# Feed-forward up projection by one level of Strassen's method, with the gated rows kept in DRAM

## The reference

```python
def conv_ffn(h, w_up, conv_w, conv_b, w_down, rows):
    bsz, length, _ = h.shape
    u = (h @ w_up).reshape(bsz, rows, length // rows, 2 * D_FF)
    up = jnp.pad(u, ((0, 0), (0, 0), (1, 1), (0, 0)))
    u = up[:, :, :-2] * conv_w[0] + up[:, :, 1:-1] * conv_w[1] + up[:, :, 2:] * conv_w[2] + conv_b
    a, b = jnp.split(u.reshape(bsz, length, 2 * D_FF), 2, axis=-1)
    return (jax.nn.silu(a) * b) @ w_down
```

## Time and profile before

| | us |
|---|---|
| median of 3 runs (2785.47 to 2792.19) | 2789.98 |
| span of the profiled execution | 2783.0 |
| from there to the median | 7.0 |
| PE busy in the span | 2719.7 |
| DVE, ACT, POOL busy | 1490.9, 1080.5, 256.6 |
| up projection, in the span | 2056.3 to about 2537.7 |

### The profile page before, as it was taken

The page is one execution under the profiler, slowest core; times in us unless marked ns, Lnnn a source line. Parts: engine busy times, 40 slices in busy tenths (PEclk is TensorE's granted clock), DMA queues, the critical chain, the costliest instruction groups (busy, mean ns, idle before and its releaser), DMA issues.

```text
span 2783.0 us, 42406 instructions
## 1 busy us (share of the span) xinstructions
PE 2719.7 (98%) x17076; PEld 2343.7 (84%) x17076; DVE 1490.9 (54%) x2652; ACT 1080.5 (39%) x2084; POOL 256.6 (9%) x392
## 2 busy tenths in 40 slices
PE   6999999999999999999999999999999999999999
PEld 6888888888998888878887988888998888888887
DVE  5766664544446566654445485553374444545335
ACT  5444443333334444433334552223362222224232
POOL 2211100000002122000002060000030000000000
PEclk9999999999999999999999999999999999999999
DMA  4211211111321212122113241113231111111113
GB/s 151 63 63 55 78 60 60 60 58 62 131 84 46 71 64 80 60 69 81 51 65 117 67 137 46 46 46 113 84 114 54 46 52 47 46 53 54 53 61 129
DMA packets 149185, 200.11 MB, mean 72 GB/s; under 512 B 8806, under 2 KB 117030, under 8 KB 148990
## 3 DMA queue, kind: packets, MB, share of 16 engines
q1 hardware_dynamic: 128064, 134.20, 15.3%
q0 software_dynamic: 20928, 63.20, 6.3%
HBM read 162.66 MB, written 32.58 MB: 70 GB/s over the span
## 4 chain that ended last, share of the span: by engine, by line
PE 90%; DVE 4%; ACT 2%; issue 2%; DMA 1%; POOL 1%; SPq 0%; DVEq 0%; ACTq 0%; POOLq 0%
PE PS L977 85%; PE PS L986 5%; DMA T<-TMP 1%; DVE AL L2243 1%; DVE WL L2200 0%; DVE ST L2372 0%; POOL TMP L2979 0%; DVE TMP L2355 0%; DVE T L2348 0%; POOL T L2976 0%; ACT top L1769 0%; ACT TMP L1608 0%; ACT TMP L1718 0%; ACT WH L1596 0%; DVE top L2385 0%
## 5 line engine op out<-in xcount | busy, mean ns | idle before, releaser
L977 PE MATMUL PS<-AH,WH 128*128 128x512 f32 (+3 forms) x2528 | 941.1, 372 | 16.9 <-DVE AL L2243 10.2
L977 PE MATMUL PS<-AL,WH 128*128 128x512 f32 (+3 forms) x2528 | 894.2, 354 | 0.0
L977 PE MATMUL PS<-AH,WL 128*128 128x512 f32 (+3 forms) x2528 | 893.6, 353 | 0.0
L977 PEld LDWEIGHTS PS<-AH,WH 128*128 128x128 f32 x2528 | 476.5, 188 | 87.7 <-issue 18.7
L977 PEld LDWEIGHTS PS<-AH,WL 128*128 128x128 f32 x2528 | 476.0, 188 | 48.1
L977 PEld LDWEIGHTS PS<-AL,WH 128*128 128x128 f32 x2528 | 477.4, 189 | 44.5 <-issue 1.0
L2200 DVE TENSOR_TENSOR WL<-W,WH 128x1024 fp32r<-128x1024 f32 x184 | 226.0, 1231 | 221.5 <-ACT WH L1596 221.4
L977 PE MATMUL PS<-WH,AH 128*128 128x256 f32 (+1 forms) x1016 | 325.1, 320 | 1.7 <-DVE WL L2200 1.7
L977 PE MATMUL PS<-WL,AH 128*128 128x256 f32 (+1 forms) x1016 | 324.4, 319 | 0.0
L977 PE MATMUL PS<-WH,AL 128*128 128x256 f32 (+1 forms) x1016 | 324.4, 319 | 0.0
L2372 DVE TENSOR_REDUCE ST<-PS 128x1 f32<-128x784 f32 (+8 forms) x272 | 188.0, 732 | 144.4 <-PE PS L977 143.8
(11 more groups left out here) (341 smaller groups left out, 3345.7 us busy)
## 6 DMA issues: line engine op xcount, KB each, us to landing
W<-in_k_w_in SPq DMA_DIRECT2D x66, 512.0 KB, 3.8
W<-in_w_ada SPq DMA_DIRECT2D x48, 512.0 KB, 4.8
W<-in_w_up SPq DMA_DIRECT2D x44, 512.0 KB, 3.8
W<-in_w_in SPq DMA_DIRECT2D x28, 512.0 KB, 3.7
W<-in_w_out SPq DMA_DIRECT2D x24, 512.0 KB, 3.5
W<-in_w_down SPq DMA_DIRECT2D x22, 512.0 KB, 3.7
R<-s_xs POOLq DMA_DIRECT2D x16, 512.0 KB, 6.5
s_adap<-AST POOLq DMA_DIRECT2D x48, 128.0 KB, 4.7
```

The lines of the kernel that those rows point to most:

```text
L977: return e.matmul(out, lhsT, rhs, start=start, stop=stop, skip_group_check=True)
```

## The change

The up projection of one j, which was [a-half columns, b-half columns] by [token half 0, token half 1] with the input columns in two halves of 4 slices, is a 2 x 2 by 2 x 2 block product. It is done with seven block products in Winograd's form in place of eight. One block product is 4 slices k times three matmuls, 12 matmuls of 512 columns.

- **Activations.** Besides the blocks a11, a12, a22 of `BH`/`BL`, four combined blocks s1 = a21+a22, s2 = s1-a11, s3 = a11-a21, s4 = a12-s2 are formed once, each with its own high and low part. POOL makes s1, s3 and the cast of a22, DVE s2 and s4 and all low parts, ACT all other high parts (`combine_in`, `combine_hi`, `combine`, `combine_sums`, `combine_rest`), slice by slice for pairs 2 and 3, in pieces of 128 x 256 with one buffer (`CMB`) for each sum.
- **Weights.** POOL forms four differences of 128 x 512 for each j (`combine_weights`), ACT and DVE split each of the seven halves (`up_split`, `up_split_lo`) four products ahead.
- **Results.** Products 1, 6, 7, 4 of one j add up in one bank, and ACT copies its state out after 1, 6 and 7 (`snap`); 2 lies in a bank of its own; 5 and 3 share a third. DVE adds C11 = snap 1 + bank of 2 and C12 = snap 6 + bank of 3 (`total`), POOL C22 = snap 7 + snap 5 (`result`). PE may not begin 6, 7, 4, 3 before the snap of 1, 6, 7, 5. Three of four convolutions now read C11, C12 and C22 in SBUF.
- **Gated rows.** SBUF no longer holds all 22. Rows go to a ring of four slots, POOL writes rows 0 to 17 to DRAM (`gs`), and reads them back when the up projection is over; the down projection takes rows 18 to 21 first.

The core of the diff ("..." marks what is left out):

```diff
+        UP_SEQ = [(0, 1), (0, 2), (1, 1), (1, 2), (2, 1), (2, 2), (0, 5), (0, 6), (0, 7), (0, 3), (0, 4)]
+        UP_SEQ += [(j, p) for j in (1, 2) for p in (6, 5, 7, 3, 4)] + [(j, p) for j in range(3, FT) for p in (1, 2, 6, 5, 7, 3, 4)]
+        UP_AHEAD = 4
...
 # tensor
+            def product(i, j, p):
...
+                if p == 6:
+                    e.wait_ge(*up_snap.at((j, 1)))
+                elif p == 7:
+                    e.wait_ge(*up_snap.at((j, 6)))
+                elif p == 4:
+                    e.wait_ge(*up_snap.at((j, 7)))
+                elif p == 3:
+                    e.wait_ge(*up_snap.at((j, 5)))
+                e.wait_ge(*w_lo.at(("up", i)))
...
+            for i, (j, p) in enumerate(UP_SEQ):
+                product(i, j, p)
                 if i == 1:
+                    tensor_norm_fill(e, "ffn", 3, [b for b in ALL if b not in live])
...
 # scalar, end of the mixer
-                split_to(WI["up", 0, 0])
+                up_split(0)
+                up_split(1)
                 ffn_fill(1)
-                split_to(WI["up", 0, 1])
                 mix_squares(3, 3)
+                combine_in(2, 0)
                 mix_root(3)
+                combine_hi(2, 0, ("s1", "s3"))
                 sum_stats(3)
-                ffn_fill(2)
+                combine_hi(2, 0, ("s2", "s4"))
+                for k in range(1, 4):
+                    combine_in(2, k)
+                    combine_hi(2, k, ("s1", "s3"))
+                    combine_hi(2, k, ("s2", "s4"))
...
 # scalar, ffn
+                up_split(2)
+                up_split(3)
+                for i, (j, p) in enumerate(UP_SEQ):
+                    if i + UP_AHEAD < len(UP_SEQ):
+                        up_split(i + UP_AHEAD)
+                    if p == 1:
...
+                        snap(j, 1, C11)
+                        if j == 0:
+                            for k in range(4):
+                                combine_in(3, k)
+                                combine_hi(3, k, ("s1", "s3"))
+                                combine_hi(3, k, ("s2", "s4"))
...
+                        elif j >= 3:
+                            gate(j - 1)
+                    elif p == 2:
+                        if j != 2:
+                            convolve(j, 0, 0)
+                    elif p == 6:
...
+                        snap(j, 6, C12)
...
+                    elif p == 3:
+                        convolve(j, 1, 1)
+                        convolve(j, 1, 0)
+                    elif p == 4:
+                        convolve(j, 0, 1)
+                    if j == FT - 1 and p in (5, 7, 3):
+                        gated_hi((5, 7, 3).index(p))
+                gate(FT - 1)
+                split_to(WI["down", 0, DOWN[0]])
...
 # vector, ffn
+                    last = j - 1
+                    if p == 1 and j >= 3:
+                        taps(last, 0, 1)
+                    elif p == 2:
+                        if j >= 3:
+                            gate(last)
+                        total(j, 11)
...
+                    elif p == 6:
+                        if j >= 3:
+                            taps(j, 0, 0)
...
+                    elif p == 5 and j >= 3:
+                        row(last)
...
+                    elif p == 3:
+                        taps(j, 1, 1)
+                        total(j, 12)
+                    elif p == 4:
+                        taps(j, 1, 0)
...
+                taps(FT - 1, 0, 1)
+                gate(FT - 1)
+                row(FT - 1)
+                split_to(WI["down", 0, DOWN[0]])
+                gated_lo(3)
...
 # gpsimd
+            for j in range(FT):
+                if j + 1 < FT:
+                    combine_weights(j + 1, True)
+                if 1 <= j <= SPILL:
+                    spill(j - 1)
+                result(j)
+                if j + 1 < FT:
+                    combine_weights(j + 1, False)
...
+            for g in range(SPILL):
+                if g >= 5:
+                    e.wait_ge(*g_in[g % 5].at(("row", g - 5)))
+                e.wait_ge(*g_out[g % 4].at(("row", g)))
+                e.dma_start(gated_row(g), gs[g]).then_inc(*g_in[g % 5].landed(("row", g)))
```

More of the change, by code:

```diff
@@ L1503, in tensor_ffn @@
[L1503 to L1514, removed]
+            place, live = {}, []
@@ L1518, in product @@
                 def product(t, k):
-                    w = WI["down", half, k - k % 2]
+                    w = WI["down", half, DOWN[k - k % 2]]
                     s = split_slot(w)
@@ new lines, in combine_hi @@
+            def combine_hi(p, k, names):
+                c = slice(256 * (p - 2), 256 * (p - 2) + 256)
+                for name in names:
+                    e.wait_ge(*(mix_p.at((name, p, k)) if name in ("s1", "s3") else mix_lo.at((name, "sum", p, k))))
+                    if p == 2 and k == 0:
+                        e.wait_ge(*stored("x1", 3))
+                        e.wait_ge(*out_mm.at(("out2", 3, 3)))
+                        e.wait_ge(*fill_tr.at(("ffn", 1, 7)))
+                    e.activation(S_HI[name][:, k, c], CMB[:, int(name[1]) - 1, :], ACT.Copy).then_inc(*mix_hi.mark((name, p, k)))
@@ L2184, in pt_evac, with up_result @@
             return PT[:, pt, part[0]:part[0] + 2, :].rearrange("p a b -> p (a b)"), bank(b)
+        def up_result(j, ab, half):
+            if (ab, half) == (0, 1):
+                return bank(banks.place.get(("up", "a", j), 0))
+            return (C11 if ab == 0 else C22 if half else C12)[:, j % 2, :]
         F_OUT = [(CV if t < 4 else TH)[:, (t // 2) % 2, 512 * (t % 2):512 * (t % 2) + 512] for t in range(8)]
@@ new lines, in combine_lo @@
+            def combine_lo(name, p, k):
+                c = slice(256 * (p - 2), 256 * (p - 2) + 256)
+                if name == "a22":
+                    e.wait_ge(*mix_p.at(("a22", p, k)))
+                    src = TBf[:, 2 * (k % 2) + 1, :]
+                else:
+                    e.wait_ge(*mix_hi.at((name, p, k)))
+                    src = CMB[:, int(name[1]) - 1, :]
+                e.tensor_tensor(S_LO[name][:, k, c], src, f(S_HI[name][:, k, c]), ALU.subtract).then_inc(
+                    *mix_lo.mark((name, p, k)))
@@ new lines, in ffn @@
+                e.wait_ge(*cw_in.at(0))
+                up_split_lo(2)
+                up_split_lo(3)
+                for i, (j, p) in enumerate(UP_SEQ):
+                    if i + UP_AHEAD < len(UP_SEQ):
+                        up_split_lo(i + UP_AHEAD)
+                    if i == 0:
+                        for k in range(4):
+                            combine_sums(3, k)
+                            combine_rest(3, k)
+                    last = j - 1
[5 more added lines that the diff above has]
+                        total(j, 11)
+                        if j < 2:
+                            taps(j, 0, 0)
+                    elif p == 6:
+                        if j >= 3:
+                            taps(j, 0, 0)
+                        elif j:
+                            taps(last, 0, 1)
+                            if j == 2:
+                                taps(j, 0, 0)
+                    elif p == 5 and j >= 3:
+                        row(last)
+                    elif p == 7 and 1 <= j <= 2:
+                        gate(last)
+                        row(last)
+                    elif p == 3:
+                        taps(j, 1, 1)
+                        total(j, 12)
+                    elif p == 4:
+                        taps(j, 1, 0)
+                    if j == FT - 1 and p in (5, 7, 3):
+                        gated_lo((5, 7, 3).index(p))
```

429 lines of the change are left out of this document (305 added, 124 removed).

## The result

| | us |
|---|---|
| before, median of 4 runs | 2790.22 |
| after, median of 4 runs (2877.39 to 2889.67) | 2884.44 |
| ratio after/before, 95% interval | 1.0338 (1.0320 to 1.0356) |
| span of the profiled execution after | 2887.9 |
| its own time | 2889.67 |

The change costs 94 us where 49 were forecast: 2884 against 2839, outside the range of 2770 to 2870. The direction was right, the size was not.

What follows compares the result with a forecast made beforehand. PE alone was taken to set the pace. Terms -62.2 + 66.5 + 29.7 + 3 + 3 + 9 = +49 us gave 2839 us, with 8 in 10 between 2770 and 2870.

Steps and rivals of the forecast that it cites:

- Part 1: Up projection: one block product in eight removed, 19.0 us of matmuls for each j, -62.2 us if PE never waits.
- Part 2: Up projection from j = 3 on: period 22.5 us against 19.0 of matmuls, PE idle 3.5 us 19 times, +66.5 us.
- the walk: One up-projection period followed over PE, ACT, DVE and POOL, from one snap of product 6 to the next: 22.5 us.
- Product 7 ends at 2.7: First step of the period: product 7 ends 2.7 us after the snap of product 6.
- the clock as a case of its own: Rival: 3.5 us idle for each j brings 1.2 GHz, product 7 takes 5.1 us, 45 more, 2884 us; chance 0.11.
- part 4: Smaller terms: clock after two long start waits +3, j = 0 to 2 +3, gap before down projection +9, spills nothing.
- Parts 3 and 4: Start of up projection: idle 3.2, 12.5, 13.1 and 0.9, +29.7 us; smaller terms add +3 clock, +3 for j = 0 to 2.
- the term for the clock: Start of up projection: lower clock likely after the two long waits, +3 us (0 to 6).
- SP's loads of `w_up` wait for splits of two j earlier, a period ahead: Up-projection weight loads: buffers come free a period ahead; listed among the terms at nothing.
- The constant: Whole kernel: median of the runs lies 7 us above the profiled span, so 2832 of span became 2839.
- The second: Rival: PE stays the bound, up-projection periods 19.0, only start and end cost, 2773 us or 2758; chance 0.17.
- The first rival: POOL's holds fall beside the up-projection chain, period 19.6, time 2785 us, no change; chance 0.12.

Runs made afterwards that it cites:

- e5: e1's order plus convolutions (b,0) and (a,1) moved behind the next j's snap of product 1, first `w_down` split ahead of the last tanh; 2790.81 us, ratio 1.0007.
- e3: Kernel after plus twelve matmuls into an unread bank ahead of product 7, in PE's wait, from j = 3 on; 2865.28 us, ratio 1.0280.
- e4: Kernel after with the start's slices overlapped and splits of pairs 2 and 3 products moved ahead of slices; 2882.55 us, ratio 1.0340.
- e10: Kernel after with e6's start alone, the order from j = 1 on unchanged; 2872.36 us, ratio 1.0303.
- e7: e6 plus 44 matmuls into an unread bank in the wait ahead of product 5 of j = 0; 2776.16 us, ratio 0.9960.
- e9: Kernel after with the first down-projection weight split moved ahead of the last tanh, gate and row; 2876.82 us, ratio 1.0322.
- e6: e5 plus a new start: first two totals early, splits between slices, POOL's j = 0 differences earlier, last transposes later, slices overlapped; 2779.85 us, ratio 0.9966.
- e1: Kernel after with tanh, gate, row and convolution (a,0) moved later in the queues, and C22 ahead of the spill; 2808.71 us, ratio 1.0079.

## Why the prediction was right or wrong

**Part 1 held, within 5 us.** e5 runs at 19.19 us for seven products with PE never idle, where the earlier trace rows gave 19.0; over 22 j that is 4 us.

**Part 2: the walk was the mechanism, and its number was 1.4 us short. The step that failed is "Product 7 ends at 2.7": it was costed at the full clock, and that is 0.9 of the 1.4.** One period of the kernel after, ACT's timeline (start, duration, what ended the wait):

```profile
2360.15 0.57 ACT L2220 ACTIVATE R<-PS 128x512 f32<-128x512 f32 x1
...
2365.49 0.60 ACT L2220 ACTIVATE R<-PS 128x512 f32<-128x512 f32 x1 [3.25 <-PE PS L1036]
...
2367.56 0.82 ACT L2233 ACTIVATE R<-R 128x512 f32<-128x512 f32 x1 [0.95 <-POOL R L3368]
...
2371.18 0.81 ACT L2233 ACTIVATE R<-R 128x512 f32<-128x512 f32 x1 [2.80 <-DVE R L3087]
...
2378.74 1.06 ACT L2240 ACTIVATE R<-R 128x1024 f32<-128x1024 f32 x1 [4.38 <-DVE R L3098]
...
2384.05 0.57 ACT L2220 ACTIVATE R<-PS 128x512 f32<-128x512 f32 x1
```

DVE's, the held ones and the tap on PSUM:

```profile
2362.92 1.22 DVE L3112 SCALAR_TENSOR_TENSOR R<-R 128x1024 f32<-128x1024 f32 x1
...
2368.41 1.36 DVE L3095 SCALAR_TENSOR_TENSOR R<-R 128x504 f32<-128x504 f32 x1 [0.34 <-ACT R L2233]
...
2373.93 1.66 DVE L3098 SCALAR_TENSOR_TENSOR R<-R 128x504 f32<-128x504 f32 x1
2375.50 1.77 DVE L3058 TENSOR_TENSOR WL<-R,WH 128x512 fp32r<-128x512 f32 x1
2377.20 0.73 DVE L3095 SCALAR_TENSOR_TENSOR R<-PS,R 128x504 f32<-128x504 f32 x1
```

POOL's five additions:

```profile
2366.24 1.29 POOL L3368 TENSOR_TENSOR R<-R 128x512 f32<-128x512 f32 x1 [1.24 <-ACT R L2220]
2367.49 1.74 POOL L3363 TENSOR_TENSOR W<-W,R 128x512 f32<-128x512 f32 x1
2373.47 1.57 POOL L3356 TENSOR_TENSOR R<-W 128x512 f32<-128x512 f32 x1 [4.25 <-DVE WL L3058]
2375.12 1.61 POOL L3358 TENSOR_TENSOR R<-W,R 128x512 f32<-128x512 f32 x1
2376.69 1.75 POOL L3359 TENSOR_TENSOR W<-W 128x512 f32<-128x512 f32 x1
```

Counted from the end of the first snap (2360.72), forecast against trace: row done 3.4 and 3.4; C22 5.7 and 6.8; convolution (b,1) 6.5 and 7.7; convolution (b,0) 9.8 and 11.3; the next tanh 17.7 and 19.1; snap of 6 22.5 and 23.9. Most of the difference, 1.1, comes in at one place and stays. The walk let C22 wait for DVE, at 4.4; but product 7 ended at 4.8 in place of 2.7, its snap at 5.4, and C22 began at 5.5. Another 0.3 comes in by convolution (b,0); behind it the steps take what was worked out, the holds of POOL and DVE on each other included.

So 19 periods took 448.4 us in place of 427.5: +20.9. Of these, e3 gave back 15.9 with the clock at 1.00. The other 5.0 are the walk's own: in e3 C22 ends at 5.6 and convolution (b,1) at 6.5, as forecast, but the low part that is held twice puts total C12 at 9.4 in place of 9.0, and the snap of 6 comes at 22.9 in place of 22.5.

The prediction had the clock as a case of its own, with a chance of 0.11, and priced it at 2.4 us a period. Its own evidence spoke for it: the earlier trace rows had the lower clock behind an idle stretch, and part 4 used it for two long waits but not for the 19 short ones. It was put aside because PE stood still longer in the earlier trace rows, but there the wait was 3.83 us, hardly more than the 3.5 forecast. This line is of the kernel before:

```profile
24.64 0.66 PE L977 MATMUL PS<-AH,WH 128*128 128x352 f32 x1 [3.83 <-DVE AL L2243]
```

In the kernel after, the clock fell behind waits of 2.9 us, in every period from j = 4 to 20:

```profile
2360.77 0.79 PE L1036 MATMUL PS<-S3H,WH 128*128 128x512 f32 x1 [2.87 <-ACT R L2220]
2384.68 0.79 PE L1036 MATMUL PS<-S3H,WH 128*128 128x512 f32 x1 [2.80 <-ACT R L2220]
```

That is 0.79 us for the first matmul behind the wait against 0.47 for the stage's first at the full clock, and a clock of 0.50, the 1.2 GHz level, in the window from 2361 to 2364. The price of 2.4 was too high: the snap of 7 begins 4.8 us after that of 6 has ended, and 3.2 in e3, so the clock made product 7 longer by 1.6, and e3 gave back 0.9 of a period; the rest passed beside the chain. That this rival's 2884 us meets the median is chance: 45 us for the clock of the periods where e3 gave back 15.9, and too little for the start.

The Trainium skill (SBUF — State Buffer, Who interferes with whom) has each hold last for the other engine's whole instruction, and the prediction noted that the period would then be 23. In the rows above the held tap of 2373.93 ends at 2375.59, so its own 0.74 us run from 2374.85, and POOL's addition is done at 2375.04; the low part of 2375.50 runs its own 0.68 from 2376.59, and POOL's is done at 2376.73. The same sum gives 0.20 for the tap of 2368.41. The trace agrees with the lock but for the last 0.14 to 0.20 us of POOL's instruction, which is what the earlier trace rows had given (0.15).

**Parts 3 and 4 failed at the start, in what stands around the slices: 22.3 us too little.** A slice was forecast at 4.7 us; POOL's begin 4.64 to 4.67 apart, where no new pair begins:

```profile
2094.15 0.74 POOL L3339 TENSOR_TENSOR R<-R 128x256 f32<-128x256 f32 x1 [2.91 <-ACT R L2156]
...
2098.82 0.72 POOL L3339 TENSOR_TENSOR R<-R 128x256 f32<-128x256 f32 x1 [2.90 <-ACT R L2156]
...
2103.46 0.72 POOL L3339 TENSOR_TENSOR R<-R 128x256 f32<-128x256 f32 x1 [2.90 <-ACT R L2156]
...
2128.49 1.26 POOL L3356 TENSOR_TENSOR R<-W 128x512 f32<-128x512 f32 x1 [17.86 <-DMA W<-in_w_up]
```

PE's waits at the start of the kernel after:

```profile
2073.22 1.99 PE L1045 MATMUL PS<-ident,R 128*128 128x128 f32 x12 [1.96 <-DVE R L2993]
2082.32 1.11 PE L1045 MATMUL PS<-ident,R 128*128 128x128 f32 x4 [7.11 <-ACT R L2156]
2087.91 0.77 PE L1036 MATMUL PS<-AH,WH 128*128 128x512 f32 x1 [4.48 <-DVE WL L3058]
2113.96 0.79 PE L1036 MATMUL PS<-AH,WH 128*128 128x512 f32 x1 [18.80 <-DVE R L3087]
```

They add up to 32.4 us against 28.8 forecast for the first three gaps, but that is partly luck: the first two gaps are 2.1 us shorter than forecast and the third is 5.7 longer, with another cause. Start and j = 0 to 2 were put at 29.7 + 3 + 3 = 35.7 us; the stage's 564.6 less 419.2 and less the 87.4 of the 19 periods leaves 58. Some 44 of these are idle time (the 47.3 above, less one wait of 3.1 that belongs to the periods): 32.4 in the four waits shown, and 11.9 in five later ones, where 0.9 + 3 had been forecast. The longest of these is

```profile
2132.35 0.80 PE L1036 MATMUL PS<-S3H,WH 128*128 128x512 f32 x1 [5.01 <-ACT R L2220]
```

About 14 us are left, for which the windows' clocks of 0.73, 0.61, 0.86 and 0.94 are the only ground seen; the term for the clock was 3. By PE's own timeline this is the term that was mis-sized most.

Two causes were not in the walk. The wait of 18.8 is for the bank that total C11 of j = 0 frees behind the slices of pair 3, and it stands in front of product (2,1), where the prediction had PE go on to (2,2) and looked only at that split. And the second weights of j = 1 came late (POOL waited 17.86 us for them), which e4 traced to the 5.01 us above. Here the sentence that failed is "SP's loads of `w_up` wait for splits of two j earlier, a period ahead": at the start there is no period ahead, the buffer comes from j = 0 itself. e10 took 10 to 14 us of all this away. How the rest divides between the slices and the lower clock stays open: e7 raised PE's activity in one of the waits only, and showed no gain.

**Part 4.** The gap was forecast at 9 and is 10.5. It is the order of the queues, as e9 shows. The spills and reloads cost PE no wait: behind the gap it has none to the end of the span, though rows took 8.2 us to land where 6.5 were assumed.

```profile
R<-s_gs POOLq DMA_DIRECT2D x18, 512.0 KB, 8.2
```

**The constant.** The 7 us between the span before and the median were taken for a constant. Here each execution's time is some 1.8 us above its own span (2889.67 and 2887.9); the rest is that executions differ. It cancels between the medians, so it costs the forecast nothing.

In sum: +49 forecast, 20.9 more in the periods, 22.3 more at the start, 1.5 more in the gap make +94. The span's +104.9 has the 9.3 us before the stage and the 2 of the down projection besides. That the +94 of this sum is also the difference of the medians is partly luck: the sum is of the profiled execution, which was the slowest of the four.

**The rivals.** The second's price, 2773 with periods of 19.0, is near what e6 takes, 2780: the buffers do give the slack, but only in another order. The first rival's period of 19.6 is e1's 19.3 to 20.0, and e1's time is 24 us above its price of 2785, about what the start was short of.

## What to carry to other kernels

A saving of matmuls is worth its time only if nothing that PE waits for stands behind work of the last iteration in another engine's queue: walk one period over all engines, then move out of the way whatever PE does not need. If the walk ends with PE idle once in each period, look in the trace for a wait about as long, cost the matmuls behind yours at the clock that it shows, and walk again, since the later step can become the chain's. Here waits of 2.9 us brought the lower clock. At a loop's start, ask for each buffer and each PSUM bank who frees it the first time; "a period ahead" does not hold there.

## What the runs showed of the hardware that was not expected

- Behind a wait of PE of 2.8 to 2.9 us, once in 24 us, the clock was 0.50 for the next 3 us in each of 17 periods (2217 to 2600 us), and matmuls of that product took 607 ns where others take 390. Behind the wait of 0.85 us in the last period (2621.6) it was 1.00. With matmuls in the wait (e3) it did not fall either.
- One DVE instruction can be held by two of POOL's in a row: a low part that takes 0.68 us alone took 3.08 (e3).
- POOL is held as well: an addition of 512 columns takes 1.29 alone and up to 1.75 beside DVE's.
